# First model: gate products in three passes of high and low parts, x through DRAM

## The reference, cut to what matters

```
h = x @ w_in[l]
(rw_p, rw_g, q_lat, kv_lat, k_pe, mla_g, conv_u, conv_g, xq, xg, merge) = split(h)
y_rwkv, y_mla, y_conv, y_mem = four branches
proj  = einsum('bsnc,ncd->bsnd', branches, w_o_branch[l])
gates = sigmoid(merge.reshape(B, S, 4, D) + b_gate[l])
out   = sum(gates * proj, axis=2) @ w_out[l]
x     = layer_norm(ALPHA * x + out, ln_g[l], ln_b[l])
```

## Time and profile before

| what | value |
| --- | --- |
| median of 3 runs | 2860.42 us (2859.85 to 2860.79) |
| span of the profiled execution | 2857.6 us, some 2.8 less than the median of the runs, which holds what lies around the first and last instruction |
| gate products, line 444 | 1024 records (512 products), 229.1 us busy |
| passes of the input products, lines 477, 478, 479 | 752 each, 212.2, 209.0 and 212.8 us busy |
| Pool busy | 1342.8 us, 47% |
| DVE busy | 1019.0 us, 36% |
| granted TensorE clock, mean | 0.986 |

### The profile page before, as it was taken

One profiled execution on the slowest core, in us unless ns is written; L12 is line 12 of the kernel. 1 busy time (PEld: TensorE's weight loads), 2 busy tenths in 40 slices (PEclk: granted clock), 3 DMA queues, 4 the chain that ended last, 5 costly groups with the idle time before them and its releaser, 6 DMA issues.

```text
span 2857.6 us, 44212 instructions
## 1 busy us (share of the span) xinstructions
PE 2737.9 (96%) x17521; PEld 2281.5 (80%) x17521; DVE 1019.0 (36%) x1586; ACT 656.3 (23%) x1220; POOL 1342.8 (47%) x608
## 2 busy tenths in 40 slices
PE   8999999999999897999999999999999999898998
PEld 7987778699777775888888778888888888776996
DVE  1752753247438333001340533002330023524237
ACT  4432212144322112000131443001130001415101
POOL 4830100067010003565646555666646666667786
PEclk9999999999999998999999999999999999999999
DMA  6556633445565444323222123222223222232453
GB/s 231 187 193 249 258 141 134 183 177 187 224 238 209 160 163 120 110 94 103 88 89 103 45 67 104 90 101 94 98 89 103 90 101 97 96 117 71 151 171 138
DMA packets 68621, 390.24 MB, mean 137 GB/s; under 512 B 19232, under 2 KB 20864, under 8 KB 22528
## 3 DMA queue, kind: packets, MB, share of 16 engines
q1 hardware_dynamic: 66640, 379.03, 37.1%
q10 hardware_dynamic: 1840, 9.18, 0.9%
HBM read 387.09 MB, written 1.10 MB: 136 GB/s over the span
## 4 chain that ended last, share of the span: by engine, by line
issue 26%; POOL 11%; POOLq 10%; PE 9%; DMA 3%; DVE 1%; SPq 1%; ACT 0%; DVEq 0%; ACTq 0%
POOL m_ws L1747 9%; POOLq L1746 7%; DMA m_ring<-in_panels 3%; PE m_bank L1913 2%; POOLq L1759 1%; PE m_bank L1830 1%; POOL m_ws L1765 1%; PE m_bank L1831 1%; PE m_bank L1832 1%; POOLq L1764 1%; PE m_bank L2046 1%; SPq L1703 1%; PE m_bank L2058 1%; PE m_bank L2009 1%; PE m_bank L2010 1%
## 5 line engine op out<-in xcount | busy, mean ns | idle before, releaser
L1830 PE MATMUL m_bank<-m_aT,m_ws 128*128 128x512 f32 (+1 forms) x1792 | 631.4, 352 | 34.8 <-DVE m_aT_low L2408 15.6
L1831 PE MATMUL m_bank<-m_aT_low,m_ws 128*128 128x512 f32 (+1 forms) x1792 | 628.0, 350 | 0.0
L1832 PE MATMUL m_bank<-m_aT,m_ws 128*128 128x512 f32 (+1 forms) x1792 | 627.7, 350 | 0.0
L1747 POOL TENSOR_TENSOR m_ws<-m_ring,m_ws 128x2048 fp32r<-128x2048 f32 x127 | 593.5, 4673 | 18.7
L1913 PE MATMUL m_bank<-m_ws,m_hs 128*128 128x512 f32 x1848 | 422.6, 390 | 3.5 <-DVE m_ws L2445 1.5
L1830 PEld LDWEIGHTS m_bank<-m_aT,m_ws 128*128 128x128 f32 x1792 | 344.9, 192 | 82.2 <-issue 23.6
L1913 PEld LDWEIGHTS m_bank<-m_ws,m_hs 128*128 128x128 f32 x1848 | 346.1, 188 | 79.4 <-issue 6.9
L383 POOL TENSOR_TENSOR m_ws<-m_ring,m_ws 128x2048 fp32r<-128x2048 f32 x48 | 221.3, 4627 | 342.4 <-ACT m_ws L910 342.4
L1831 PEld LDWEIGHTS m_bank<-m_aT_low,m_ws 128*128 128x128 f32 x1792 | 345.1, 193 | 42.4
L1832 PEld LDWEIGHTS m_bank<-m_aT,m_ws 128*128 128x128 f32 x1792 | 344.9, 192 | 42.6
L2451 DVE TENSOR_TENSOR m_hidT<-m_sg,m_bank 128x512 f32 (+3 forms) x88 | 54.7, 621 | 687.6 <-ACT m_sg L2218 687.6
(11 more groups left out here) (350 smaller groups left out, 3412.9 us busy)
## 6 DMA issues: line engine op xcount, KB each, us to landing
m_ring<-in_panels SPq DMA_DIRECT2D x350, 1024.0 KB, 4.9
m_rows<-m_gg_dram ACTq DMA_DIRECT2D x6, 1024.0 KB, 5.4
m_bias<-in_rpb SPq DMA_DIRECT2D x48, 64.0 KB, 2.7
m_ring<-in_panels SPq DMA_DIRECT2D x4, 512.0 KB, 5.4
m_hT<-in_ln_rows ACTq DMA_DIRECT2D x2, 1024.0 KB, 6.8
m_con<-in_con SPq DMA_DIRECT2D x1, 1536.0 KB, 10.7
memT_ctx<-in_memT SPq DMA_DIRECT2D x2, 512.0 KB, 5.6
x_tok<-in_x SPq DMA_DIRECT2D x1, 1024.0 KB, 13.6
```

The lines of the kernel that those rows point to most:

```text
L1747: nc.gpsimd.tensor_tensor(ws[:, p, 1, :], ring[:, p, :], ws[:, p, 0, :].bitcast(F32), ALU.subtract)\
L1830: mm(out, w, a, start=start, stop=False)
L1831: mm(out, w, a_low, start=False, stop=False)
L1832: return mm(out, w_low, a, start=False, stop=stop)
```

## The change

- `gate` takes three passes for each product, 24 per 128 output columns and half panel where there were 8 products: `gate_hi` times `xT`, `gate_hi` times `xT_low`, and the low part times `xT`.
- Pool makes these parts by half panels (u = 0, 1): a one-element add behind the waits, a tensor_scalar (times 1.0) into `gate_hi[:, u]`, and a subtract that writes the low part over the panel in its ring slot (`ring_low` is the same memory as `ring`). Half 0 of a gate waits for half 0 of the gate before it to be used (`gate_unit`), half 1 for the whole of the gate before it; both for the panel's landing. PE waits for each half (`gate_split`).
- `xF` and its add go. Pool's four memsets move from behind the attention to behind the split of gate (6, 1).
- `xT_low` now lies over `x_tok` and `gate_hi` over `memT`. So ACT saves x to DRAM at the layer's start (`x_out`), DVE writes `xT_low` only when that is done and x is transposed, and ACT brings x (`x_back`) and `memT` (`mem_in`) back behind gate (1, 1). DVE's line 1454 waits for `x_back`, PE's first product of a layer for `mem_in`, and SP for the last `mem_in` before it loads `ctx`.

```diff
@@ gpsimd
-                pool.wait_ge(s["panel_used"], l * PANELS1 + PANEL[("in", 23)] + 1)
-                nc.gpsimd.tensor_tensor(xF[:, :, :], xT[:, :, :].bitcast(F32), xT_low[:, :, :].bitcast(F32), ALU.add)\
-                    .then_inc(s["xF_in"], 1)
-                pool.wait_ge(s["o_done"], 4 * l + 4)
...
+                for at, (q, p) in enumerate(GATES):
+                    n = PANEL[("gate", q, p)]
+                    pool.wait_ge(slot[n % RING], (l * (PANELS1 // RING) + n // RING + 1) * 16)
+                    for u in range(2):
+                        if at == 0:
+                            pool.wait_ge(s["panel_used"], l * PANELS1 + PANEL[("mem", 3)] + 1)
+                        elif u == 0:
+                            pool.wait_ge(s["gate_unit"], l * len(GATES) + at)
+                        else:
+                            pool.wait_ge(s["panel_used"], l * PANELS1 + PANEL[("gate",) + GATES[at - 1]] + 1)
+                        nc.gpsimd.tensor_tensor(idle, idle, idle, ALU.add)
+                        pool.drain()
+                        nc.gpsimd.tensor_scalar(gate_hi[:, u, :, :], w[:, u, :, :], 1.0, 0.0, ALU.mult, ALU.add)
+                        pool.drain()
+                        nc.gpsimd.tensor_tensor(w_low[:, u, :, :], w[:, u, :, :], gate_hi[:, u, :, :].bitcast(F32),
+                                                ALU.subtract).then_inc(s["gate_split"], 1)
+                    if (q, p) == (6, 1):
...
@@ tensor, gate(q, p)
                     for u in range(2):
+                        pe.wait_ge(s["gate_split"], l * 2 * len(GATES) + 2 * GATES.index((q, p)) + u + 1)
                         for k in range(KD):
-                            last = mm(out[:, u * T:(u + 1) * T], w[:, u, k, :], xF[:, k, :], start=(k == 0), stop=(k == KD - 1))
+                            mm(dst, gate_hi[:, u, k, :], xT[:, k, :], start=(k == 0), stop=False)
+                            mm(dst, gate_hi[:, u, k, :], xT_low[:, k, :], start=False, stop=False)
+                            last = mm(dst, w[:, u, k, :], xT[:, k, :], start=False, stop=(k == KD - 1))
+                        if u == 0:
+                            last.then_inc(s["gate_unit"], 1)
@@ scalar
+                    if n == 0:
+                        act.wait_ge(s["x_in"], l + 16)
+                        act.dma_start(x_dram[...], x_tok[...]).then_inc(s["x_out"], 16)
...
                 gate(1, 1)
+                act.dma_start(x_tok[...], x_dram[...]).then_inc(s["x_back"], 16)
+                act.dma_start(memT, io["memT"]).then_inc(s["mem_in"], 16)
@@ vector
+                dve.wait_ge(s["x_out"], 16 * (l + 1))
+                dve.wait_ge(s["xT_ps"], 4 * l + 4)
...
+                        dve.wait_ge(s["x_back"], 16 * (l + 1))
```

More of the change, by code:

```diff
@@ L145 @@
 stream_of_a_layer()
+GATES = [name[1:] for name in PANEL if name[0] == "gate"]
 ALPHA = (2.0 * DEPTH) ** 0.25
@@ L325, in first_model @@
             "rv_ps rv_in mt_ps mt_in zt_ps zt_in y_ps y_in st_ps st_in ysq_in ystd_req ystd_in yn_in yt_ps yaff_in rw_done sig_in merged "
-            "half_ps zeros_in k_sb xF_in var_in ln_var ln_std layer_done").split()}
+            "half_ps zeros_in k_sb x_out x_back gate_split gate_unit var_in ln_var ln_std layer_done").split()}
         slot = [s["slot0"], s["slot1"], s["slot2"], s["slot3"]]
@@ L391, in _ @@
-                for rows, n in ((slice(0, 64), 1), (slice(0, 64), 3), (slice(64, 128), 0), (slice(64, 128), 2)):
-                    nc.gpsimd.memset(AR[rows, :, :, n, :], 0.0).then_inc(s["zeros_in"], 1)
+                for at, (q, p) in enumerate(GATES):
+                    n = PANEL[("gate", q, p)]
+                    w = ring[:, n % RING, :].rearrange("p (u k c) -> p u k c", u=2, k=KD)
+                    w_low = ring_low[:, n % RING, :].rearrange("p (u k c) -> p u k c", u=2, k=KD)
+                    pool.wait_ge(slot[n % RING], (l * (PANELS1 // RING) + n // RING + 1) * 16)
[13 more added lines that the diff above has]
+                    if (q, p) == (6, 1):
+                        pool.wait_ge(s["o_done"], 4 * l + 4)
+                        nc.gpsimd.tensor_tensor(idle, idle, idle, ALU.add)
+                        pool.drain()
+                        for rows, half in ((slice(0, 64), 1), (slice(0, 64), 3), (slice(64, 128), 0), (slice(64, 128), 2)):
+                            nc.gpsimd.memset(AR[rows, :, :, half, :], 0.0).then_inc(s["zeros_in"], 1)
+                        pool.drain()
@@ L438, in gate @@
                 def gate(q, p):
-                    w = panel(("gate", q, p)).rearrange("p (u k c) -> p u k c", u=2, k=KD)
+                    panel(("gate", q, p))
+                    w = ring_low[:, PANEL[("gate", q, p)] % RING, :].rearrange("p (u k c) -> p u k c", u=2, k=KD)
                     out = free(("gate", q, p))
                     for u in range(2):
+                        pe.wait_ge(s["gate_split"], l * 2 * len(GATES) + 2 * GATES.index((q, p)) + u + 1)
+                        dst = out[:, u * T:(u + 1) * T]
                         for k in range(KD):
-                            last = mm(out[:, u * T:(u + 1) * T], w[:, u, k, :], xF[:, k, :], start=(k == 0), stop=(k == KD - 1))
+                            mm(dst, gate_hi[:, u, k, :], xT[:, k, :], start=(k == 0), stop=False)
[3 more added lines that the diff above has]
+                            last.then_inc(s["gate_unit"], 1)
                     last.then_inc(s["panel_used"], 1)
@@ L488, in transpose_x @@
                             last.then_inc(s["xT_ps"], 1)
-                pe.wait_ge(s["mem_in"], 16)
+                pe.wait_ge(s["mem_in"], l * 16 + 16)
                 pe.wait_ge(s["first_in"], l * 16 + 16)
@@ L1087, in _ @@
                 gate(1, 1)
+                act.dma_start(x_tok[:, :, :].rearrange("p i d -> p (i d)"),
+                              x_dram[bass.ds(l, 1), :, :].rearrange("o p n -> p (o n)")).then_inc(s["x_back"], 16)
+                act.dma_start(memT, io["memT"]).then_inc(s["mem_in"], 16)
                 mod_columns(8)
@@ L2625, in program @@
     with ExitStack() as ctx:
+        with ExitStack() as place:
+            xT_low = place.enter_context(nc.sbuf_tensor("m1_xT_low", [P, KD, T], F32R))
         x_tok = ctx.enter_context(nc.sbuf_tensor("x_tok", [P, NT, D], F32))
@@ L2629, in program @@
                  "con": ctx.enter_context(nc.sbuf_tensor("m1_con", [P, NCON], F32)),
-                 "mem": ctx.enter_context(nc.sbuf_tensor("memT_ctx", [P, NT * D], F32)),
                  "loaded": ctx.enter_context(nc.semaphore("m2_loaded"))}
+        with ExitStack() as place:
+            early["gate_hi"] = place.enter_context(nc.sbuf_tensor("m1_gate_hi", [P, 2, KD, P], F32R))
+        early["mem"] = ctx.enter_context(nc.sbuf_tensor("memT_ctx", [P, NT * D], F32))
+        early["xT_low"] = xT_low
         first_model(nc, io, x_tok, mod, early)
```

15 lines of the change are left out of this document (8 added, 7 removed).

## The result

The changed kernel takes 2916.6 us (median of 4 runs, 2915.6 to 2917.3), the kernel before, run beside it, 2860.1: ratio 1.0199, 95% interval 1.0185 to 1.0214, slower by 56.5 us. The forecast was 2924, 64 slower. The profiled execution spans 2913.0 us, 55.4 more than the earlier trace rows.

What follows compares the result with a forecast made beforehand. PE and DVE were both taken as bounds from attention's end to the transposes. Per layer 5.5 + 28 - 1.6 = 32 us, two layers 64; 2857.6 + 2.8 + 64 = 2924, range 2885 to 2955.

Steps and rivals of the forecast that it cites:

- Part 1: Gate matmuls: three passes at 0.118 us make a panel 5.65 us, 1.45 less; 32 panels free 46 us of PE.
- not held, and landings covered: Rival: the 11 gates outside DVE's chain save 1.45 us each, 16 per layer: 2828; chance 0.05.
- Attention, +5.5 a layer: Six gates in attention: PE waits for Pool's splits of late-landing panels, so attention ends 5.5 us later per layer.
- End of attention to transposes, +28: DVE's 63 us chain: Pool's split halves hold DVE, eight for 3.6 us each, making it 28 us longer per layer.
- A wait of 10 to 25 us at line 662: Sign of being right: at the transposes PE waits 10 to 25 us for DVE in each layer.
- PE waiting for Pool more than for DVE: Sign of being wrong: PE's waits for Pool exceed its waits for DVE; no size given.
- A chain of about 91 us: Sign of being right: DVE's chain from L1269 to L1343 becomes about 91 us long.
- Transposes to branch(0), -1.6: Recurrence to the gate stage's end: five shorter gates give -7.2 us, +5.6 is given back, net -1.6 per layer.
- Part 3: Moving x and memT through DRAM: all transfers are covered by other work and cost 0.
- DVE keeps its turn: Rival: Pool gets in only at gaps between DVE's queued instructions, half the holding goes, 18 us per layer: 2896; chance 0.15.
- No holding: Rival: Pool's half-length instructions don't stop DVE, the chain keeps its length, -1.9 us per layer: 2857; chance 0.06.
- slow passes: Rival: gate passes take 0.15 us instead of 0.118, 1536 passes cost 49 us more: 2973; chance 0.02.

Runs made afterwards that it cites:

- no_split2: Changed kernel with Pool making only the first gate's high part each layer and no panel split, same three passes, third with xT_low as weights: 2832.2 us, ratio 0.9899.
- fill: Changed kernel with 8 to 42 short matmuls on PE ahead of its waits for Pool in seven half panels of each layer: 2914.4 us, ratio 1.0192.
- memset_split2: Changed kernel with Pool's tensor_scalar and subtract of each half replaced by four memsets of about the same total length, gate weights constant: 2883.6 us, ratio 1.0086.
- hold_alone2: Kernel before, with only Pool running ten add, tensor_scalar and subtract groups on memT per layer during DVE's chain: 2897.3 us, ratio 1.0129.
- tail_passes: Changed kernel with twelve gates a layer back in full precision, only the four beside the recurrence in three passes, high parts by ACT: 2859.2 us, ratio 0.9995.
- dram_alone2: Kernel before, with only x saved to DRAM and brought back, memT loaded again, and the waits for these: 2859.5 us, ratio 0.9998.
- hold_scalar: Kernel before, with Pool running ten groups a layer of a one-element add and three one-input tensor_scalars during DVE's chain, no subtract: 2883.7 us, ratio 1.0090.
- hold_late: Kernel before, with ten add, tensor_scalar and subtract groups on Pool per layer, held back until DVE's chain is through: 2874.1 us, ratio 1.0042.

## Why the prediction was right, point by point

The sign and the two mechanisms (DVE held by Pool, PE waiting for the split) were right. That 64 came so near to 56.5 is partly luck: over the two layers I had 11 us for attention and the runs show 25.0 (14.4 + 10.6), and I had 56 for the chains and they grew by 34.6. The two errors, +14 and -21, largely cancel. The tails (-3.2, measured -4.2) add little.

- *Part 1, a pass of 0.118, 46 us of PE freed.* Right: at full clock a pass starts every 0.12 us. What shows of it without a split is 28 us (no_split2, 2832), where "not held, and landings covered" had worked out 2828.
- *Attention, +5.5 a layer.* Undersized: +14.4 in layer 0, about +10.6 in layer 1. The step that failed is the timetable of landings, with the clock behind the waits. Gate(4,0) waited 5.33 (I had 3.9 + 1.4). But gate(5,1), predicted to end at 258.6, began at 255.25 and ended at 263.57: its panel was requested at 240.4, not 239.2, and landed 8.7 later, at the slow end of the earlier trace rows, where I had carried the 6.5 of the earlier trace rows over. That DVE's softmax multiply would stand in Pool's way there was right (Pool's one-element add took 2.27 us at 249.24). In layer 1 the same gate waits only 3.1 and 1.3. Gates (2,1), (7,0) and (1,1) wait for their splits in the same way (2.6, 5.0 and 3.1). The passes behind the waits ran at the lower clock (gates of 7.8 and 8.3 us for 5.65), which I had left out; by fill it is worth about 2 us in all. memset_split2, with hardly any holding, shows that the splits' length makes most of the term: its chain starts 11.0 late.
- *End of attention to transposes, +28.* Right in kind and shown alone by hold_alone2; oversized: +17.3. I had put eight halves at 3.6 each. The trace of the changed kernel has all ten in the chain, but a half holds DVE for 2.7 to 3.0 where it meets two-operand instructions all along: the four beside L1308, L1323 and L1326 cost 5.9 + 0.7 + 4.65 = 11.2. (6,1), which I had laid beside the first reciprocal, ran from 361 to 370, behind it and partly beside instructions that read PSUM, and cost 2.4. (7,0) and (7,1) cost 6.3 together; a good part of them lies beside the second reciprocal (382.92 to 389.45), where nothing is held. DVE's waits shrank by 2.5 us, about as forecast, and 11.2 + 2.4 + 6.3 - 2.5 is the 17.3 measured, to 0.1. "Each stands still for the other's whole length" holds for the instruction that arrives just then, not for a whole half.
- *A wait of 10 to 25 us at line 662.* Wrong: 4.8 and 4.5 (L420). PE was late itself: in the same stretch it waits for Pool in gates (6,0) and (7,0) (2.1, 3.5 and 5.0 in layer 0) and for DVE behind `branch(3)` (L444, 1.8 and 4.3), which I had not seen as a second meeting place. hold_alone2 shows 9.3 there and 5.6 at the transposes.
- *"PE waiting for Pool more than for DVE" as a sign of being wrong.* It came true, 51.5 us against 15.3, although the chain did grow. The wait of PE was a bad measure of what DVE costs, since a PE that is late for another reason hides it. It does point to the term I had too small: the split's length costs 51 us of the 84, holding 33.
- *A chain of about 91 us:* 80.65, the same error as above.
- *Transposes to branch(0), -1.6.* Right in size: 135.1 against 136.9 in layer 0. tail_passes suggests part of why no better was to be had there: a gate is cover for DVE's work in the recurrence.
- *Part 3 at nothing.* Right for the transfers: dram_alone2.
- *"DVE keeps its turn", 2896.* Its mechanism is ruled out by the rows: the instructions of L1326 are queued without a wait, and Pool's get in between them (12.38 for 7.73). Its size for the chain, +14, was nearer than mine all the same; its time was not. *"No holding"* is ruled out by hold_alone2, and *slow passes* by no_split2.

The Trainium skill, SBUF — State Buffer, section Who interferes with whom, had named the tensor_scalar as held too, which no row of the kernel before showed. L1342 (2.67 for 0.69) and hold_scalar's L1302 (1.53) now do. By the same section a Pool memset should leave DVE's two-operand instructions alone, and memset_split2's chain agrees (64.4 against 80.7), with its tensor_scalars as the part that is held.

## What to carry to other kernels

Before giving work to an idle GpSimd, look at what VectorE does in the same microseconds: beside reciprocals and instructions with an operand in PSUM it cost nothing here; beside instructions with two SBUF operands a half of 3.4 us cost DVE about 2.8, and Pool's subtract up to 0.9. And price a hand-over by its latency: a gate that becomes 1.45 us shorter is no gain when 3.9 us of preparation per half stand between the landing of its data and its first pass. When a chain of one engine is level with PE, shorter PE work beside it gains little until that chain is shorter too. And give every sign in a forecast a cause of its own: a wait says how late one engine is against another, not what the other costs.

## What the hardware showed that I had not expected

- The clock differs over identical work. In hold_late nothing is changed ahead of the first chain, and gate(4,0) has the same 1.43 us wait as in the earlier trace rows:

```profile
206.31 8.86 PE L458 MATMUL m_bank<-m_xF,m_ring 128*128 128x256 f32 x32 [1.43 <-DMA m_ring<-in_panels]
```

It takes 8.86 us instead of 7.17, with a granted clock of 0.83 against 1.00 in 200 to 210 us. The first chain starts at 306.15, 306.28, 308.17, 310.45 and 311.87 in the kernel before, hold_scalar, tail_passes, hold_late and hold_alone2, all with the same gates ahead of it (in tail_passes reading x from another place). What tips it stays open. Differences of up to 5.7 us between the first layers of two profiles can be this, so such a difference is no evidence for an edit.
- Both engines pay, one instruction at a time: Pool's subtract takes 2.35 alone and up to 3.26 beside the chain, its one-input instruction 1.04 alone and 1.82 in hold_scalar; DVE's six of L1326 take 12.38 for 7.73.
- DVE's reciprocal (6.53 to 6.55 us over 1024) holds nobody and is not held: between 382.92 and 389.45 Pool's pair ran at 1.05 and 2.38.
